# Last pair's up weights in two halves, and another order and place for the last sums, in a two-layer decoder trunk with a mixture of experts

## The reference

```python
def hierarchical_moe(hn, w_group, b_group, w_router, b_router, w_gate, w_up, w_down):
    ...
    gates = jnp.sum(jax.nn.one_hot(expert_id, N_EXPERTS, dtype=F32) * top_w[..., None], axis=1)
    ...
    for grp in range(N_GROUPS):
        a = jnp.einsum("nd,edf->nef", t, w_gate[grp])
        u = jnp.einsum("nd,edf->nef", t, w_up[grp])
        act = jax.nn.silu(a) * u * gates[:, grp, :, None]
        y = y + jnp.einsum("nef,efd->nd", act, w_down[grp])
...
    for layer in range(DEPTH):
        hn = rmsnorm(h, attn_norm[layer])
        ...
        h = h + hierarchical_moe(rmsnorm(h, ffn_norm[layer]), ...)
    return rmsnorm(h, final_norm)
```

## Time and profile before

| | us |
|---|---|
| median of 3 runs | 1095.43 |
| lowest and highest | 1093.26, 1098.76 |
| the profiled execution, its time | 1096.88 |
| the profiled execution, its span in the profile | 1095.0 |

### The profile page before, as it was taken

The page is one execution under the profiler, slowest core; times in us unless marked ns, Lnnn a source line. Parts: engine busy times, 40 slices in busy tenths (PEclk is TensorE's granted clock), DMA queues, the critical chain, the costliest instruction groups (busy, mean ns, idle before and its releaser), DMA issues.

```text
span 1095.0 us, 12899 instructions
## 1 busy us (share of the span) xinstructions
PE 1001.8 (91%) x5140; PEld 575.4 (53%) x5140; DVE 386.8 (35%) x1103; ACT 233.9 (21%) x605; POOL 91.6 (8%) x103
## 2 busy tenths in 40 slices
PE   5999999999998999999788998899999999998866
PEld 3344644455455656666434647536455666665532
DVE  3123621336145323222243316547225333222215
ACT  3122620236011000000022216537202100000002
POOL 2000000000101011211101001000100111111100
PEclk9999999999999999999999999999999999999998
DMA  9522205964336999999999420023624899999996
GB/s 330 215 91 76 77 2 174 210 266 168 120 125 228 407 420 419 420 419 419 421 348 334 165 77 1 11 77 154 237 96 168 325 420 419 421 418 420 416 374 226
DMA packets 63549, 276.95 MB, mean 253 GB/s; under 512 B 12787, under 2 KB 17379, under 8 KB 38906
## 3 DMA queue, kind: packets, MB, share of 16 engines
q1 hardware_dynamic: 53088, 256.95, 60.9%
q0 software_dynamic: 10400, 19.16, 5.0%
HBM read 261.94 MB, written 30.44 MB: 267 GB/s over the span
## 4 chain that ended last, share of the span: by engine, by line
PE 66%; DMA 20%; DVE 5%; SPq 3%; issue 2%; ACT 2%; POOL 1%; POOLq 0%; DVEq 0%; ACTq 0%
PE bank L841 13%; PE bank L931 10%; PE bank L1054 9%; PE bank L853 9%; DMA K<-rows,small 7%; PE bank L872 5%; PE bank L1068 5%; DMA D<-in_moe_w_down 5%; DMA hnT<-in_moe_w_down 3%; PE bank L883 3%; DMA W<-in_moe_w_up 2%; PE bank L899 2%; SPq L449 2%; PE bank L1241 2%; DMA oT<-in_o_w_in 1%
## 5 line engine op out<-in xcount | busy, mean ns | idle before, releaser
L841 PE MATMUL bank<-hnT,W 128*128 128x512 f32 x336 | 145.1, 593 | 0.8 <-ACT hnT L1334 0.8
L1068 PE MATMUL bank<-D,PT 128*64 128x512 f32 x416 | 105.1, 611 | 10.1 <-DMA D<-in_moe_w_down 7.4
L841 PEld LDWEIGHTS bank<-hnT,W 128*128 128x128 f32 x336 | 63.5, 190 | 80.5 <-issue 79.5
L1054 PE MATMUL bank<-W,PT 128*64 128x256 f32 x640 | 78.6, 386 | 13.0 <-DMA W<-in_moe_w_up 6.7
L1759 DVE SCALAR_TENSOR_TENSOR PT<-bank,small,PT 128x256 f32<-128x256 f32 x32 | 15.5, 484 | 210.8 <-PE bank L1054 210.8
L1781 DVE SCALAR_TENSOR_TENSOR K<-K,small,bank 128x512 f32<-128x512 f32 x64 | 47.8, 747 | 86.7 <-PE bank L1068 86.5
L1054 PE MATMUL bank<-W,cst 128*64 128x256 f32 x640 | 77.5, 381 | 0.0
L872 PE MATMUL bank<-K,Q 128*128 128x256 f32 (+3 forms) x256 | 70.4, 417 | 6.1 <-ACT K L1353 3.4
L853 PE MATMUL bank<-W,hnT 128*128 128x512 f32 (+2 forms) x256 | 71.4, 439 | 0.0
L1368 ACT ACTIVATE P<-P,nm 128x256 f32<-128x256 f32 (+3 forms) x128 | 68.3, 535 | 14.6 <-DVE nm L1551 14.1
L1408 ACT ACTIVATE PT<-bank 128x256 f32<-128x256 f32 x32 | 12.3, 384 | 271.9 <-PE bank L1060 271.9
(11 more groups left out here) (245 smaller groups left out, 1364.1 us busy)
## 6 DMA issues: line engine op xcount, KB each, us to landing
D<-in_moe_w_down SPq DMA_DIRECT2D x48, 1024.0 KB, 22.8
W<-in_moe_w_gate SPq DMA_DIRECT2D x40, 1024.0 KB
W<-in_moe_w_up SPq DMA_DIRECT2D x40, 1024.0 KB, 19.6
hnT<-in_moe_w_down SPq DMA_DIRECT2D x12, 1024.0 KB, 17.7
W<-in_e_w_in SPq DMA_DIRECT2D x5, 2048.0 KB
expert_rows<-K SPq DMA_DIRECT2D x2, 4096.0 KB, 34.8
V<-in_moe_w_gate SPq DMA_DIRECT2D x6, 1024.0 KB
Q<-in_moe_w_gate SPq DMA_DIRECT2D x6, 1024.0 KB
```

What stands on the lines that cost most here:

```text
L841: last = nc.tensor.matmul(b[:, :], w[:, k, 128 * fb:128 * fb + 128], hnT[:, k, :], start=(k == 0), stop=(k == KD - 1))
L1054: last = nc.tensor.matmul(bank[b][at, 0:256], XT[k // 4][:, k % 4, at], w[:, 256 * k:256 * k + 256], start=(k == 0), stop=(k == KD - 1))
L1068: last = nc.tensor.matmul(bank[5 + half][at, :], hT[:, 128 * c + 64 * a:128 * c + 64 * a + 64], d[:, col:col + 512], start=(c == 0), stop= ...
```

## The change

Five things change. The up weights of the last pair are sent as four transfers of half an expert each, the first halves of the contraction of both experts before the second ones; a new semaphore `s_ulast` counts the first halves, and the up product waits for each half where it comes to it. DVE's `finish` of the last pair moves from ahead of `add_expert_rows` into it, behind `add_row(0)`. In layer 0 the norm of chunk 0 goes ahead of `add_row(1)`. In layer 1 DVE now adds the rows of chunks 0, 1 and 2, and TensorE those of chunk 3, where it was 0 and 3 on DVE, 1 and 2 on TensorE. On TensorE in layer 0 `transpose_second(0)` comes behind the combination of chunk 3 instead of ahead of it.

```diff
-        summed = [(), (1, 2)]
+        summed = [(), (3,)]
...
+        s_ulast = sem("last_ups_first_halves_loaded")
...
                     sp.wait_ge(s_gu, free)
-                    load_half(lay, 2 * p, 1)
-                    load_half(lay, 2 * p + 1, 1)
+                    if p < NP - 1:
+                        load_half(lay, 2 * p, 1)
+                        load_half(lay, 2 * p + 1, 1)
+                    else:
+                        for part in range(2):
+                            for e in (2 * p, 2 * p + 1):
+                                up = expert_slot(lay, e)[0][1]
+                                half = slice(DM * part, DM * part + DM)
+                                sp.dma_start(up[:, half], wu_v[lay][e][:, half])\
+                                  .then_inc((s_ulast, ups_landed(lay, p)[0])[part], 16)
...
                 def ups(p):
                     pair = pair_slots(p)
-                    pe.wait_ge(*ups_landed(lay, p))
-                    product(3, [slot[0][1] for slot in pair], lambda half: None).then_inc(s_gu, 1)
+                    landings = [ups_landed(lay, p)] * 2
+                    if p == NP - 1:
+                        landings[0] = s_ulast, 32 * (lay + 1)
+                    product(3, [slot[0][1] for slot in pair], lambda half: pe.wait_ge(*landings[half])).then_inc(s_gu, 1)
...
                 for c in range(C):
-                    if c == 3 and lay == 0:
-                        transpose_second(0)
                     last = late_product(lay, c)
...
+            transpose_second(0)
             latent_rows(0)
...
                 add_row(0)
+                finish(lay, NP - 1)
                 add_late(0)
                 if lay == 0:
+                    norm_chunk(2, 0)
                     add_row(1)
-                    norm_chunk(2, 0)
                     add_late(1)
...
                 else:
+                    add_row(1)
+                    add_late(1)
                     norm_chunk(4, 0)
-                    add_late(1)
-                    add_row(3)
+                    add_row(2)
+                    add_late(2)
                     norm_chunk(4, 1)
-                    add_late(2)
                     add_late(3)
...
             further_tiles(0)
-            finish(0, NP - 1)
             add_expert_rows(0)
```

More of the change, by code:

```diff
@@ L1973, in _ @@
             further_tiles(1)
-            finish(1, NP - 1)
             add_expert_rows(1)
```

## The result

The changed kernel takes 1098.60 us in the median of 20 runs (1096.18 to 1101.70) against 1097.37 for the kernel before (1093.26 to 1098.93, 20 runs beside them). The ratio on record is 1.0018, with a 95% interval of 1.0009 to 1.0026. That is 2.0 us more; the two medians by themselves lie 1.2 us apart. Either way it is within the 0.5% that I called no change and at the slower side of it. The forecast was 1.4 us more and a time of 1096.8, from a median before of 1095.43; over 20 runs that median is 1.9 us higher.

The account below looks back on a forecast made before the run. TensorE is busy for 91% of the span; the change touches only the chain of waits ending each layer's expert stage. Layer 1's +1.75 and layer 0's -0.35 make +1.4 us on 1095.43: 1096.8 us, range 1093.0 to 1099.6.

Parts of the forecast that it names:

- Up weights by halves: End of layer 1: first halves land some 2.5 us before the last piece; the down product ends 2.3 us sooner.
- Row 0 ahead of finish: End of layer 1, DVE: finish waits for row 0's landing and sum, starting 0.3 us later; the 2.3 us are lost.
- The clock: Layer 1, chunk 0's combination: after 2.65 us of TensorE idleness the clock falls, +1.7 us, with bounds 0 and 1.7.
- The sums: Layer 1: DVE adds chunks 1 and 2, TensorE chunk 3; this gives back 0.25 us by the last norm.
- Layer 0: End of layer 0: chunk 0's copy ends later, the projection's slow start goes; between -1.7 and +1.3, taken as -0.35 us.
- The sum: Whole kernel: layer 1 +1.75 with the clock's fall and layer 0 -0.35 make +1.4 us, so 1096.8 us.
- the signs that I had named for a wrong forecast: finish released by TensorE in both layers, or chunk 0's rows landing later than 1074.5 or earlier than 1072.
- the signs for the profile after: Among them: layer 0's projection still released by its weights, within 0.5 us of 576.98, and shorter than 8.80.
- Rival (b): The gain arrives: row 0 lands over 2.5 us earlier, finish follows the down product; 1092.8 us, chance 0.2.
- Rival (c): Slower: layer 0's sums come out from behind the projection's weights, its slow start stays; 1098.5 us, chance 0.15.
- (d): The splitting does nothing: pieces land together, only layer 1's sums and layer 0's -0.35 stay; 1095.1 us, chance 0.1.
- Slow pieces: Smaller transfers delay all queued behind, row 0 too: up to 3.4 us, leading past 1100.9; chance 0.05.

Follow-up runs that it names:

- the second set: The changed kernel unaltered, run once more against the kernel before, with a second profile: 1098.22 us, ratio 1.0008.
- the run with layer 0 as before: The changed kernel with layer 0's order of finish, row sums, norm and transposes as in the kernel before, halves kept in both layers: 1097.48 us, ratio 1.0002.
- the kernel with halves and sums: The kernel before plus up weights by halves and layer 1's new places of the sums, finish first and layer 0 in old order: 1095.37 us, ratio 0.9986.
- the kernel with halves only: The kernel before with the up weights of the last pair sent by halves and nothing else: 1095.99 us, ratio 1.0000.

## Why the prediction was right

**Up weights by halves: right, 2.3 us forecast.** With the halves alone the distance from row 0 to the first combined sum shrank by 2.4 us. But "the first halves some 2.5 us before the last piece" is one case among others: the wait ahead of the second half's product was 0.30 to 3.33 us in the nine profiles with halves, and over 2.5 us in four of them.

**Row 0 ahead of finish: right.** Forecast: the sum was free behind the combination, the row's landing takes its place, and `finish` is held until 1.3 us after it. The profile after has 1.26 us in both layers, and DVE released by the transfer. Taking the move back gave 2.3 us by the ratios (1.2 against the second set), and a second row ahead of `finish` cost 7.2.

**The clock: right in size, not in its certainty.** I took 1.7 us. Where a fall covers all four records, the first combined sum starts 3.5 us after the combination instead of 2.06, so the fall is 1.45 us; with the 0.27 by which `finish` starts later behind the landing this makes the 1.72 in the distance from the landing. The clock fell in both layers in both profiles of the changed kernel, and not in layer 1 of the run with layer 0 as before, after 3.01 us. I had read a limit between 2.25 and 2.52 us out of two rows. The other profiles don't bear it out. The projection of layer 0 after 1.94 us of idleness in the kernel with halves and sums, and after 2.70 us in the kernel with halves only:

```profile
577.13 8.80 PE L862 MATMUL bank<-oT,hnT 128*128 128x512 f32 x16 [1.94 <-DMA oT<-in_o_w_in]
```

```profile
576.32 7.11 PE L862 MATMUL bank<-oT,hnT 128*128 128x512 f32 x16 [2.70 <-DMA oT<-in_o_w_in]
```

The first is slow and the second is not. The length of one idle time does not decide it.

**The sums: right in sign, too small.** The term was -0.25 us; it is -1.0. I had laid DVE's instructions end to end with 0.04 us between them. In the profile the next one starts up to 0.08 us before the last one ends wherever it follows a combined sum or a norm (1080.85, 1.29 us long, then 1082.06). Five such joints up to the last combined sum make 0.6 us of the difference of 0.8; the rest lies behind that sum, in ScalarE's part and the last norm.

**Layer 0: the term was -0.35 us, and it is +0.5 and +1.3 in the two profiles.** The fall that went away from the projection is there (8.80 to 7.10), and the copy is the new releaser, as forecast for the case with a fall. DVE's copy came to 578.93 where the forecast had 578.2 with a fall, and in the second profile ScalarE's copy, behind TensorE's combinations and transposes, released the projection at 579.95. What was off is mainly the landing of row 0. I took 564.55 from the one execution; over the twelve profiles it lies between 564.5 and 566.6, so I had the earliest of all.

**The sum.** Layer 1, from row 0's landing to the last norm: +0.7 us (forecast +1.75). Layer 0: +0.5 (forecast -0.35). The remaining 1.0 of the 2.1 us between the two profiles lies between the two places. The stretch from the end of layer 0's first projection to the issue of layer 1's row 0 is 480.2 us before and 481.5 in the changed kernel, and row 0's own transfer gives 0.4 back (7.4 us for 7.8). What goes with the longer stretch in all twelve profiles is the down product at about 1047 us, shown with the profile after. In six profiles it took 3.65 us, after 2.1 to 3.2 us of idleness, and in these the stretch is 479.7 to 480.3 us. In the other six, the changed kernel's two among them, it took 5.1 to 6.5 us at a lower clock, after 2.3 to 3.2 us of idleness, and the stretch is 481.1 to 482.5. The change touches neither that product nor its weights. It was slow in six of the nine profiles with halves and in none of the three without, so whether the halves have a part in it stays open.

So the mechanism was right, and that the size came out close is in part luck: +1.4 forecast and 1.2 to 2.0 measured, with the sums of layer 1 and layer 0 each off by 0.8, in opposite ways, and a microsecond from a product that the forecast did not look at.

One of the signs that I had named for a wrong forecast did come: a landing of row 0 in layer 1 later than 1074.5. It landed at 1075.18, and at 1076.73 in the second profile, because it was issued 1.8 and 2.4 us later than before; that down product, 2.8 and 1.5 us longer than before, lies ahead of both. Two others of the signs for the profile after failed in layer 0: the projection was not released by its weights, and not within 0.5 us of 576.98. The account of layer 1 is not touched by this, since `finish` follows the landing wherever it comes.

Rival (b), that the gain arrives, did not come: in both profiles of the changed kernel row 0 landed after the last down product had ended, in both layers. Rival (c) is half of what happened: layer 0 did come out from behind the weights, but the projection's slow start went. (d) is refuted by the halves alone: in no profile with them did the pieces land together, the first half's product ran first. Slow pieces are not what costs: with the pieces in place and `finish` first the time is that of the kernel before or better. A loss under a microsecond stays open, since row 0 of layer 1 lands 7.4 to 9.6 us after its issue in the nine profiles with pieces and 7.8 to 8.2 in the three without. The Trainium skill's fit for one transfer ("DMA: Bandwidth & Descriptors", section Anatomy of one DMA, for transfers issued by GpSimd) makes it 4 us, an estimate; no run here shows a loss of that size from the 512 KB pieces, which SP issues and which stand queued behind other transfers.

## What to carry to other kernels

Before a sum is moved ahead of something that another engine waits for, ask what it is free behind now, and what its own input waits for: a cheap instruction in an in-order queue carries its wait to all that stand behind it. A wait that is shortened at one link of a chain is worth only the distance to the next link that is late, and the time won there turns into idle time of the engine in between, in which its clock may fall. When parts of a change point in opposite ways, each a few microseconds, try them one by one: here two parts, the halves and the sums, are together 1.5 us faster than the kernel before, and the move of `finish` in layer 1 by itself takes 1.8 us of it back.

## What the runs showed of the hardware that I had not expected

The landing of one transfer, in the same place of the same program, varies by more than the whole effect: row 0 of layer 1 lands 7.4 to 9.6 us after its issue, row 0 of layer 0 5.7 to 8.3. The second halves of the up weights came 0.3 to 3.3 us after TensorE was ready for them. And 3.01 us of idleness left the clock up (the run with layer 0 as before), while 1.94 us let it fall (halves and sums). One product of 3.65 us, in the same place of the program, took up to 6.5 us in other executions, and it goes with over a microsecond of difference between two profiles that is easily taken for an effect of the edit.
